# RWKV's decays, a, kk, b, k and the turned values computed beside the projections; the scan's outputs moved between banks and steps

## The reference, cut to what matters

```python
z = z + mu * (centred_shift(z) - z)
r, k, v, w_lo, a_lo, g_lo = split(z)                   # 512,512,512,128,64,128
w_log = -softplus(-(w0 + tanh(w_lo) @ w_up)) - 0.5     # two directions
decay = exp(-exp(w_log))                               # = exp(-c*sigmoid(...))
a  = sigmoid(a0 + a_lo @ a_up)
kk = k * k_k;  kk = kk * rsqrt(max(sum_head(kk * kk), 1e-24))
k  = k * (1 + (a - 1) * k_a);  b = kk * a
y  = scan(r, decay[0], k, v, kk, b) + scan reversed(r, decay[1], k, v, kk, b)
# a step of the scan: sa = S @ -kk; S = S*w + sa (x) b + v (x) k; y = S @ r
```

## Time and profile before

| | us |
|---|---|
| median of 3 runs | 3775.36 |
| lowest, highest | 3765.24, 3780.02 |
| the profiled execution | 3766.57 |
| its span | 3765.3 |
| TensorE busy, matmuls | 3310.5 (88%) |
| DVE busy | 2288.5 (61%) |
| ACT busy | 988.5 (26%) |
| mean granted TensorE clock | 0.931 |

### The profile page before, as it was taken

The page is one execution under the profiler, slowest core; times in us unless marked ns, Lnnn a source line. Parts: engine busy times, 40 slices in busy tenths (PEclk is TensorE's granted clock), DMA queues, the critical chain, the costliest instruction groups (busy, mean ns, idle before and its releaser), DMA issues.

```text
span 3765.3 us, 56674 instructions
## 1 busy us (share of the span) xinstructions
PE 3310.5 (88%) x24667; PEld 2740.1 (73%) x24667; DVE 2288.5 (61%) x3161; ACT 988.5 (26%) x1464; POOL 367.6 (10%) x202
## 2 busy tenths in 40 slices
PE   7988798568787699999999987998888989999997
PEld 5777686367777477888888766885776768888885
DVE  5758565447776444444444466897555566666666
ACT  4543142121110222111111244112455221211212
POOL 2510043000000300000000021000001011111110
PEclk9988698589998799999999999998999989999999
DMA  4410154111211212111111202113001011111111
GB/s 136 131 31 11 43 171 125 50 41 29 37 33 24 99 56 62 51 51 43 42 51 51 95 29 68 51 44 93 1 1 53 23 43 45 56 45 45 56 45 62
DMA packets 261824, 209.29 MB, mean 56 GB/s; under 512 B 87000, under 2 KB 223975, under 8 KB 260935
## 3 DMA queue, kind: packets, MB, share of 16 engines
q1 hardware_dynamic: 247751, 180.50, 16.3%
q10 hardware_dynamic: 13824, 25.17, 2.2%
HBM read 172.84 MB, written 30.95 MB: 54 GB/s over the span
## 4 chain that ended last, share of the span: by engine, by line
PE 70%; DVE 17%; ACT 5%; DMA 2%; SPq 2%; issue 2%; POOL 2%; DVEq 0%; ACTq 0%; POOLq 0%
PE ps L1925 22%; PE ps L1940 15%; PE ps L1788 5%; PE ps L617 4%; PE ps L619 4%; PE ps L618 4%; PE ps L1362 2%; PE ps L2673 2%; DVE Yc L2550 2%; DVE s_Z L1531 2%; DVE s_tmp L1530 2%; PE ps L2649 2%; SPq L1336 1%; PE ps L672 1%; PE ps L2659 1%
## 5 line engine op out<-in xcount | busy, mean ns | idle before, releaser
L2967 DVE TENSOR_TENSOR H<-H,ps 128x1024 f32<-128x1024 f32 x256 | 312.7, 1221 | 181.4 <-PE ps L1940 174.6
L2090 DVE TENSOR_TENSOR fsum<-fsum,ps 128x1024 f32<-128x1024 f32 x168 | 205.2, 1221 | 312.5 <-PE ps L1940 310.4
L1940 PE MATMUL ps<-dh,hh 128*128 128x512 f32 x864 | 340.7, 394 | 20.3 <-DVE hl L1905 14.3
L1940 PE MATMUL ps<-dl,hh 128*128 128x512 f32 x864 | 339.1, 392 | 0.0
L1940 PE MATMUL ps<-dh,hl 128*128 128x512 f32 x864 | 338.9, 392 | 0.0
L1925 PE MATMUL ps<-hn_h,uh 128*128 128x512 f32 x704 | 276.4, 393 | 7.0 <-DVE ul L1629 4.6
L1925 PE MATMUL ps<-hn_h,ul 128*128 128x512 f32 x704 | 276.0, 392 | 0.0
L1925 PE MATMUL ps<-hn_l,uh 128*128 128x512 f32 x704 | 276.0, 392 | 0.0
L1925 PE MATMUL ps<-hx_h,uh 128*128 128x512 f32 x512 | 201.6, 394 | 7.8 <-DVE hx_l L1905 5.3
L1940 PEld LDWEIGHTS ps<-dh,hh 128*128 128x128 f32 x864 | 163.8, 190 | 58.1 <-DVE hl L1905 15.9
L1925 PE MATMUL ps<-hx_l,uh 128*128 128x512 f32 x512 | 201.3, 393 | 0.0
(11 more groups left out here) (474 smaller groups left out, 7670.0 us busy)
## 6 DMA issues: line engine op xcount, KB each, us to landing
aw<-in_w_ada_dram ACTq DMA_DIRECT2D x96, 256.0 KB, 2.9
uw<-in_w_mlp_dram SPq DMA_DIRECT2D x32, 512.0 KB, 4.3
dw<-in_w_mlp_dram SPq DMA_DIRECT2D x32, 512.0 KB, 5.2
uw<-in_ffn_gate_dram SPq DMA_DIRECT2D x22, 512.0 KB, 4.0
uw<-in_ffn_up_dram SPq DMA_DIRECT2D x22, 512.0 KB, 5.4
dw<-in_ffn_down_dram SPq DMA_DIRECT2D x22, 512.0 KB, 6.0
cw<-in_w_in_dram SPq DMA_DIRECT2D x20, 512.0 KB, 3.9
o_w<-in_w_out_dram SPq DMA_DIRECT2D x16, 512.0 KB, 13.2
```

Of the source, the lines that this page charges most:

```text
L1940: mm = pe.e.matmul(ps[:, 2 * pair + hf, :], v[s][:, blk(t)], w[:, half(hf)], start=(m == 0), stop=(m == 2))
L2090: return dve.c.tensor_tensor(f, f, new, ALU.add) if g else dve.c.tensor_copy(f, new)
L2967: return dve.c.tensor_tensor(h, h, self.ps[:, 4 + 2 * (t % 2):6 + 2 * (t % 2), :], ALU.add)
```

## The change

- The preparation stage is gone. Its pieces are jobs (`RJOBS`) hung between the half blocks of the projections, `(j, h)` meaning after half `h` of block `j`; they use banks 6 and 7. The order of the blocks is now w_lo, a_lo, g_lo, k, v, r; r overwrites v's place once v is turned and stored.
- The weights' raw and low parts have a ring of three; a load waits for the matmuls of the block three before.
- Squares of kk and `1 + (a-1) k_a` move from DVE to ACT. `w_lo` and `a_lo` stay in place, their trip through DRAM is gone; the decay matmul contracts over 64 rows instead of 128 with zeros.
- Constants, the first `sig`, V's turn, the first `cum_pe` and the first exponentials are issued inside the projections' stage; the `meet` calls `rwkv_prep` and `rwkv_const` are gone. POOL clears ZZ and B after the last block, S after the meet.
- Scan: outputs use bank 2, so they no longer wait for S; direction 0's stand before the transposes, direction 1's after p4 on TensorE and after t4 on DVE. p4, p5, l5 are in bank 1, l4 in bank 0. Four of the eight ZZ loads are issued by ACT, four by SP.

```diff
+    RJOBS = {(2, 1): ("sg", 0), (3, 0): ("sg", 1), (3, 1): ("sg", 2), (4, 0): ("sg", 3), (4, 1): ("sg", 4), (5, 0): ("sg", 5), (5, 1): ("sg", 6), (6, 0): ("sg", 7),
+             (6, 1): ("av", 0), (7, 0): ("av", 1), (7, 1): ("kk_sums", 0), (8, 0): ("over", 0), (8, 1): ("over", 1), (9, 0): ("over", 2), (9, 1): ("over", 3),
+             (10, 0): ("av", 2), (11, 0): ("VT", 0), (12, 0): ("VT", 1), (13, 0): ("VT", 2), (14, 0): ("VT", 3), (14, 1): ("av", 3)}
...
+    def rwkv_job_pe(self, kind, n):
+        pe, act, dve, ps = self.pe, self.act, self.dve, self.ps
+        if kind == "sg":
+            pe.wait_ge(self.t_misc["r_small"], act["r_wlo"], dve["sg", n - 1] if n else act["xr_inv"])
+            for d in range(2):
+                rows = slice(CH * d, CH * d + CH)
+                mm = pe.e.matmul(ps[:, 6 + d, :], self.r_wlo[rows, blk(n)], self.r_wup[rows, :], start=True, stop=True)
...
+        elif kind == "kk_sums":
+            pe.wait_ge(act["kk_sq", 3], act["av", 1])
...
+        elif kind == "over":
+            if n:
+                pe.wait_ge(dve["kk", n - 1])
+            self.over_pe("kk%d" % n, NBLK, self.r_kw[n % 2])
...
         self.split_pe("r", self.rw, blocks, self.xs_at, lambda j: self.dve["r_read", j], self.plain_order(blocks), {}, after)
+        self.pe.wait_ge(self.t_misc["r_const"], self.act["av", 3])
+        self.cum_pe(0)
         self.ada_sum_pe(11)
+        self.pe.wait_ge(self.dve["gain", 2])
+        for r, src in enumerate((self.gain[:, 0, :], self.mod[:, 16:24, 0], self.gain[:, 2, :], self.mod[:, 40:48, 0])):
+            tr = self.pe.e.transpose(self.ps[0:DC, 5, blk(r)], src, self.ident[:])
...
+        sp.wait_ge(self.pe["r", 14], self.dve["r_sh", 14])
+        sp.e.dma_start(self.eye16[:].rearrange("p d b c -> p (d b c)"), i["k_eye16"]).then_inc(*self.t_misc.one("r_const"))
+        sp.wait_ge(self.dve["mod_rows"])
+        sp.e.dma_start(self.dram["rows"].rearrange("r (c p) -> c r p", p=PART), self.mod_rows[:].rearrange("c (r p) -> c r p", p=PART)) \
+            .then_inc(*self.t_b[0].one("rows"))
...
+            elif 4 <= j < 8:
+                c = j - 4
+                act.wait_ge(dve["r_sh", 3 + c])
+                act.e.activation(self.kk[:, c, :], self.rkv[:, 4 + c, :], ACTF.Square, scale=self.col("rwkv_k_k", c)).then_inc(*act.one("kk_sq", c))
```

The scan's side, on TensorE, SP, ACT and DVE:

```diff
+            def outputs(d):
+                self.heads_pe(d, 2, CH, 0, ((lambda l, H: S[H, l, :], lambda l, H: AR[H, l, 1, :]), (v, lambda l, H: MM[H, l, 1, :]),
+                                            (lambda l, H: self.U[H, l, :], lambda l, H: NM[H, l, 1, :])), "yy", u, d)
             if u >= 0:
-                for d in range(2):
-                    pe.wait_ge(dve["S", u, d])
...
+                outputs(0)
...
-                pe.wait_ge(self.t_z["in", m])
+                pe.wait_ge(self.t_z["in", m], self.t_zb["in", m])
...
+                    self.heads_pe(d, 1, CH, 0, ((lambda l, H: NM_m[H, l, 0, :], lambda l, H: ZZ[H, l % 4, l // 4, 0, :]),), "p4", m, d)
+            if u >= 0:
+                outputs(1)
...
-            for k in range(8):
+            self.inverse_back(sp, self.t_z, n, range(0, 8, 2))
...
+            if 0 <= u + 1 < NSUB:
+                act.wait_ge(self.t_z["out", u + 1])
+                if u >= 1:
+                    act.wait_ge(pe["l4", u - 1, 1], dve["zz", u - 1, 1])
+                self.inverse_back(act, self.t_zb, u + 1, range(1, 8, 2))
...
             if u >= 0:
-                for d in range(2):
...
+                outputs(0)
             if u + 3 < NSUB:
                 products(u + 3)
             if u >= 0 and m < NSUB:
+                dve.wait_ge(dve["S", u, 1])
...
+            if u >= 0:
+                outputs(1)
```

More of the change, by code:

```diff
@@ L226, in __init__ @@
         self.t_lat = [self.transfer(f"t_lat{k}") for k in range(2)]
+        self.t_zb = self.transfer("t_zb")
         self.t_x = [self.transfer(f"t_x{k}") for k in range(3)]
@@ L395, in plan_block1 @@
[L395 to L401, removed]
+        put = self.put
@@ new lines, in rwkv_in_sp, with store @@
+        for d in range(2):
+            sp.e.dma_start(self.r_wup[CH * d:CH * d + CH, :], i["rwkv_w_up"][0, d]).then_inc(*self.t_misc.one())
+            sp.e.dma_start(self.r_w0[:, d, :], i["rwkv_w0"][0, d:d + 1, :].to_broadcast([PART, RW])).then_inc(*self.t_misc.one("r_small"))
+        def store(job):
+            if job and job[0] == "sg":
+                n = job[1]
+                sp.wait_ge(self.act["sg", n])
+                sp.e.dma_start(sg[0, n], self.r_sg[n % 2][:, 0]).then_inc(*self.t_r[n].one())
+                sp.e.dma_start(sg[1, NBLK - 1 - n], self.r_sg[n % 2][:, 1]).then_inc(*self.t_r[n].one("sg", n))
@@ new lines, in rwkv_in_sp @@
+        for j in range(15):
+            store(self.RJOBS.get((j, 0)))
+            if j + 3 < 15:
+                self.third_load_sp("r", self.rw, blocks, j + 3)
+            if j == 4:
+                sp.wait_ge(self.act["r_sglo"])
+                sp.e.dma_start(self.dram["lo"][2], self.r_sglo[:]).then_inc(*self.t_st.one("lo"))
+            store(self.RJOBS.get((j, 1)))
+            if 8 <= j < 12:
+                x = j - 8
+                sp.wait_ge(self.dve["r_sh", 7 + x])
+                sp.e.dma_start(self.dram["v"][:, x, :], self.rkv[:, x, :]).then_inc(*self.t_k[x].one("v", x))
@@ new lines, in rwkv_in_sp @@
+        sp.wait_ge(self.pe["r", 14], self.dve["r_sh", 14])
[3 more added lines that the diff above has]
+            .then_inc(*self.t_b[0].one("rows"))
+        self.meet(sp, "rwkv_in", self.t_st["lo"], self.t_b[0]["rows"], *(self.t_k[x]["v", x] for x in range(4)))
@@ new lines, in rwkv_in_pe, with follow @@
+    def rwkv_in_pe(self):
+        blocks, after = self.rwkv_blocks(), {}
+        groups = dict(zip((3, 5, 6, 8, 10, 11, 13), range(4, 11)))
+        def follow(j, h):
+            if (j, h) == (0, 1):
+                self.over_pe("xr", NBLK, self.r_sh[0][:])
+            if h and j in groups:
+                self.ada_sum_pe(groups[j])
+            if (j, h) in self.RJOBS:
+                self.rwkv_job_pe(*self.RJOBS[j, h])
+        for j in range(15):
+            for h in range(2):
+                after[j, h] = lambda j=j, h=h: follow(j, h)
@@ L1317, in rwkv_scan_sp @@
[L1317 to L1323 removed]
+        self.meet(dve, "rwkv_in")
@@ L1376, in rwkv_scan_pe @@
         pe, act, dve, ps = self.pe, self.act, self.dve, self.ps
-        self.meet(pe, "rwkv_const", self.t_misc["r_const"])
-        for b in range(NSUB):
-            for x in range(4):
-                for H in H01:
-                    tr = pe.e.matmul(ps[H, b // 2, (b % 2) * 256 + x * CH:(b % 2) * 256 + (x + 1) * CH], self.rkv[H, 8 + x, b * CH:(b + 1) * CH],
-                                     self.eye[H, :], start=True, stop=True)
-        tr.then_inc(*pe.one("VT"))
-        pe.wait_ge(act["VT"])
-        self.cum_pe(0)
         for u in range(-2, NSUB):
```

393 lines of the change are left out of this document (207 added, 186 removed).

## The result

The changed kernel takes 3727.6 us (median of 4, 3721.6 to 3732.4) against 3770.8 before: ratio 0.988, 95% interval 0.986 to 0.991. It is faster by 43 us where 87 to 91 were forecast, and lies above the range of 3672 to 3700. The profiled execution took 3725.4 us, its span is 3724.0.

A forecast was written before the change was run, and what follows sets the result against it. It took TensorE to bound the projections, a chain of waits the preparation, and a TensorE-DVE chain with transfers the scan. 3766.6 - 83.6 (preparation) - 5 (scan) = 3678 for the profiled execution; it gave 3684, range 3672 to 3700.

The forecast's parts named there:

- Preparation, -83.6: Between the last projection matmul and the scan: 146.0 us become 43 of added jobs plus a 19.4 tail, saving 83.6.
- a stage longer by over 55: Stated sign of a wrong forecast: the projections' stage, expected 43 us longer, growing by over 55.
- 16.3 if the clock falls: Sums of kk squared in the projections: 9.5 us in all at a good clock, 16.3 at a fallen one.
- 2.5 with the hand-overs: Projections, before the sums of kk: TensorE waits 2.5 us for ACT's fourth square, hand-overs included.
- fewer rows to contract change nothing: Decay jobs in the projections: columns stay the same, so each job costs 1.71 us, 13.7 for eight.
- z = T + 5.9: Scan step: with four loads per queue, ZZ is in (z) 5.9 us after the substitution's end (T).
- the first rival: Scan: the ZZ loads don't get faster, ZZ staying at 8.2 us after the substitution; 3719 us, chance 0.17.
- engines busy by a third: Scan: the transfers' engines are busy only a third of the time while ZZ comes in, supporting the low 5.9.
- l4 at z + 5.4: Scan step: l4 starts 5.4 us after ZZ is in, through p4, second outputs, DVE's products and t4.
- The outputs' move buys nothing by itself: Scan: moving the outputs exchanges a wait of 2.7 us a step for another of the same size.
- The jobs cost more: Rival: projection jobs exceed their issue time (clock +7, ACT's queue +8), some scan steps at half clock; 3700 us, chance 0.11.
- The scan gains: Rival: ZZ is in at 5.4 us (-7) and TensorE keeps its clock without the wait for S (-7); 3670, chance 0.07.

## Why the prediction was wrong

The medians make a ladder from the kernel before to the changed one, an edit a rung:

| kernel | us | rung |
|---|---|---|
| before | 3771 | |
| new preparation, old scan | 3703.7 | -67 |
| ZZ loads split | 3694.5 | -9 |
| outputs in bank 2, no wait for S | 3676.8 | -18 |
| p4, l4, p5 in their new banks | 3678.4 | +2 |
| second sum of outputs behind t4 | 3673.8 | -5 |
| second outputs behind p4 (the changed kernel) | 3727.6 | +54 |

The intervals of these times are 6 to 11 us to either side, so the rungs of 9, 2 and 5 show nothing by themselves. Those of 67 and 54 stand clear, and that of 18 has the step's 1.5 us beside it. The kernels ran on several chips, on which the kernel before differs by 0.5 us.

- *Preparation, -83.6: measured -67, of which the stage itself 72.* The tail was near (17.0 for 19.4), though one term of its sum doesn't follow from its source: eight of the records at 13.81/64 are 1.7, not 1.3. The forecast's own sign of being wrong, a stage longer by over 55, came: it is 57.0. Of the jobs, the sums of kk failed, in the two figures that the forecast kept as "16.3 if the clock falls" and "2.5 with the hand-overs": 13.8 us for 7.0, and a wait of 7.2. The wait is late work of ScalarE: five pieces of `w_ada_2` paced by POOL, then a's sigmoid, the factor, a split and the square, which ends at 573.8 where block 7 ended at 566.7. With the decays' waits for VectorE (3.8, forecast none) and some 2.6 at half clock in block 8 the misses are 18; 14 of them show. The other 4 are about what the decays won: a job was priced at 1.71, with "fewer rows to contract change nothing", and takes 1.13 with its tail, about 4 to 5 us less over the eight. Four records of the same shape take 1.98 in the job of `a`; the difference nearest at hand is that the decays' two directions stand on different halves of the 128 rows. The price at full clock was taken from a row of 16 sums and applied to a row of 64. That parts of 16 between full blocks run at full clock, four times over, the spread sums show; what a row of 64 does alone is shown but for the 1.76 us ahead of it, and that rows of 24 did it four times with no wait near speaks for the row.
- *z = T + 5.9 and the first rival.* The split works: T + 6.2 in the changed kernel, 28 us in the kernel with the outputs early. That the time lies near this rival's 3719 is chance; its mechanism did not come about. The Trainium skill's sentence (DMA: Bandwidth & Descriptors, section Issuing engines are not separate DMA queues), that only the sequencer's time is saved, fits these rows; that this is usually small does not: it was 1.5 us of the 8.0 to p4. The row for "engines busy by a third" ends ahead of the last landings; in the changed kernel the share is 0.72 while TensorE waits for ZZ, and the loads land in time all the same.
- *l4 at z + 5.4, the failed step.* The mechanism was named and found where it was said to be: VectorE waits for the second outputs, which stand behind p4. Its size was wrong twice. The outputs behind p4 were priced at full clock and ran at 0.54 in the step shown, and t4 and l4 behind them at 0.50: l4 at z + 6.5, T + 12.7 in place of 11.3. That the 3.4 us of idling for ZZ bring the clock down there fits the order of the rows; no run isolates it. And what follows l4 was taken from the kernel before, less the wait for N16, 16.3 us; it was 18.1 (30.8 - 12.7), of which the first 5 us ran at a clock of 0.50 to 0.56 in the step shown. The wait for N16 did go, as forecast. Together 3.1 us a step, 39 over the scan: the 39.7 of the first section.
- *"The outputs' move buys nothing by itself: a wait of 2.7 us a step is exchanged for another of the same size."* It is not an exchange. Taking the outputs off S is worth 18 us, putting the second behind p4 costs 54. The two are separate edits, and priced apart they could have shown the loss. The forecast compared the new l4 with the old one, not with the one that the freed chain would have had (T + 8.2).
- *Rivals.* "The jobs cost more" came about in the projections, "half clock into a few steps" in all of them; it had 0.11 and ended at 3700, without the longer part behind l4. "The scan gains" came about in the kernels with the outputs early. The clock that the scan was to keep, because TensorE no longer waits for S, it lost (0.87 for 0.92): the idle time moved from 2.7 us a step ahead of the outputs to one piece of 3.4 us ahead of p4 and one of 2.9 ahead of l4 in the step shown (before 1.2 and 1.3).

Open: how much of the 18.1 us behind l4 is the clock and how much the chain; with the outputs early it is still 17.8 at a clock of 0.90, before it was 17.3 with waits for N16 in it. A hint: from l4 to the next substitution the two kinds of steps take 10.5 and 7.0 us at a clock of 0.81 and 0.71 in the changed kernel, and 9.3 and 6.3 at 0.98 and 0.95 in the one with the second products behind t4, which differs in VectorE's order too.

## What to carry to other kernels

When a producer is moved behind an instruction that waits for a transfer, everything that waits for the producer waits for the transfer too: look for its readers, buffer releases among them, before counting the slot as free. Price the two halves of a move (off the old wait, onto the new one) apart, and compare with the best order that the first half allows, not with the old time. Short matmuls are cheap here in pieces of 16 between long ones; in one row of 64 they cost twice, and part of the block behind them with them, and 24 in a row did so at times.

## What was not expected of the hardware

- Within 2 us of the start of a row of 64 matmuls of 2 columns, each with 128 columns of weights, the granted clock falls from 1.00 to 0.50, although TensorE is busy all the time by the row's records (1.76 us of waiting stand ahead of it): 12.6 us for 64, against 1.84 for 16 between full blocks, four times over. At the end of 24 such matmuls in a row, with no wait near, it fell in four of six cases. The Trainium skill (TensorE: Matmul & The Clock Gate, section What's actually happening) ties the clock to how busy TensorE has been; here its records have no gap and the clock falls all the same.
- Eight loads issued from one queue in 4.7 us cost 1.5 us more to p4 than four and four. The landings take 1.8 to 3.4 us, median 2.1, in the changed kernel, against 1.9 before and 1.9 in the changed kernel with one queue: two queues cost some 0.2 us of landing.
- A step of the scan gets 4.7 us shorter for 4.5 us by which l4 starts earlier; in the opposite sense, with one queue, 2.4 us of l4 cost 2.4 us a step. Behind l4 the step is nearly rigid, 17.1 to 18.1 us in every kernel here.
